# Two-block mixer and expert kernel: gate columns of the second block as fp32 products in four column tiles

## The chip, the cores and the metric

The kernel runs on one core of one Trainium2 chip. The metric is the device time of one execution in microseconds, the median of several. Before the change it is 902.6 us (902.14 to 905.36 over three runs).

## The reference

Two blocks over 256 tokens of 1024 features. The first (an RG-LRU and a spatial gating unit, then a hierarchical mixture of 32 experts) isn't touched. The second has two layers; each projects the normalised tokens to 4360 columns and mixes them by attention, retention and an mLSTM. The last 8 of the columns are the input and forget gates of the mLSTM's four heads:

```python
def hybrid_layer(x, norm_w, w_in, ...):
    h = rmsnorm_2(x, norm_w)
    proj = jnp.matmul(h, w_in).astype(jnp.float32)
    (aq, ak, av, ag, bq, bk, bv, bg, cq, ck, cv, co, cg, ci, cf) = jnp.split(proj, cuts, axis=-1)
    ya = merge_heads(moba_attention(aq, ak, av)) * jax.nn.silu(ag)
    yb = head_norm(retention(rotate(bq), rotate(bk), bv), ret_norm_w) * jax.nn.silu(bg)
    qk = jax.nn.silu(causal_dwconv(jnp.concatenate([cq, ck], axis=-1), conv_w, conv_b))
    i_pre = ci.transpose(0, 2, 1) + gb[:C_HEADS][None, :, None]
    f_pre = cf.transpose(0, 2, 1) + gb[C_HEADS:][None, :, None]
    # mlstm takes the cumulative sum of log_sigmoid(f_pre) over the tokens
    yc = mlstm(qk[..., :C_WIDTH], qk[..., C_WIDTH:], cv, i_pre, f_pre) * jax.nn.sigmoid(co)
    yc = head_norm(yc, mlstm_norm_w) * jax.nn.silu(cg)
    return x + jnp.matmul(jnp.concatenate([ya, yb, yc], axis=-1), w_out)
```

The code is cut: splitting into heads, padding and types are left out. `ci` and `cf` are the gate columns, 4352 to 4359.

## The kernel before

One core, each engine with its own queue written out by hand; semaphores order the engines among each other, and an engine runs its queue strictly in order. After the experts (until about 591 us) comes the second block, `second_block`, with the functions `second_sp`, `second_pe`, `second_act`, `second_pool` and `second_dve`, each of them looping over the layers l = 0, 1.

The projection's weights lie in HBM as "units" of 256 columns, 22 a layer with the output matrix (`NU`). A unit holds 8 row blocks (k = 0 to 7) of 128 rows. Features lie on partitions, tokens on the free axis: `xT` is 8 x (128 x 256). To multiply in fp32r with near fp32 precision each operand is split: ScalarE copies a piece of the weights to a rounded high half (`high(l, u)`, line 1358), VectorE subtracts it from the original to get the low half (`low(l, u)`, line 1366), both in the order of the list `PIECES`; `high(l, u)` and `low(l, u)` do all pieces up to unit u that aren't done yet. The tokens, scaled by the norm's weights, are split in the same way to `HH` and `HL`. TensorE then does three fp32r products for each k (line 1476). `tile(l, u, j)` is 128 columns of unit u, 24 products of 128x128 weights with 256 tokens. The norm's per-token factor comes later, from `rs`, when results leave PSUM.

Unit 2 (`U_ROWS`) holds the gate columns: 8 real ones, padded to 128 (input gates at columns 0 to 3, forget gates at 32 to 35). It is loaded as 128 columns (512 KB), halved like the others (piece `(U_ROWS, 0)`) and multiplied in `tile(l, 2, 0)`. Its result is read by VectorE's `gate_chain` (line 2038 on, lines 2041 and 2042 first), which computes log-sigmoid, cumulative sum and running maximum on 4 partitions. The chain's end (line 2064) is what `stabilisers` on TensorE (lines 1563 and 1564) waits for.

The order of work around it, in each layer. TensorE: the pair of units 0 and 1 (8 steps), the sums of squares (line 1541), `spread_pe` (line 1558, which waits for the root's diagonal `rt` of VectorE, line 2206), `tile(l, 2, 0)`, unit 3 (`U_CO`) in two halves, units 4 and 5 by token (`by_token`, line 1500), unit 6's first half, `stabilisers`, unit 6's second half, `m_rows`, and so on to `r_scores` (line 1635, four 32-row tiles at once), the attention values by token (units 10 and 11, line 1500 again) and the output. ScalarE in layer 0: `high(0, 3)`, the root of the norm (line 1811), `high(0, 5)`, `gate_start`. In layer 1: `high(1, 2)`, the root, `high(1, 5)` (so the halves of unit 3 and then of 4 and 5), `gate_start`. VectorE in layer 0: `low(0, 3)`, the root's reciprocals and diagonal, the copy of the spread factor to `rs` (line 2211), two `conv_in` (line 2251), `low(0, 4, 0)`, two steps of the gate chain, `low(0, 4)`, and so on. In layer 1: `low(1, 2)`, reciprocal and diagonal, `low(1, 3)`, `turn_squares` (four 32x32 transposes of the residual, line 2265), the copy to `rs`, and then as in layer 0. SyncE reloads a unit's slot when the unit four before it is done (`s_unit`).

## Time and profile before

| | |
|---|---|
| median of 3 runs | 902.6 us |
| span of the profiled execution | 901.9 us |
| TensorE busy | 855.3 us (95%) |
| VectorE busy | 416.6 us (46%) |
| ScalarE busy | 301.7 us (33%) |
| second block | from about 591 us to the end |

In the profile PE is TensorE, PEld its weight loads, DVE VectorE, ACT ScalarE, SP SyncE. A group names its line, engine and operation, the tile written and the one read, and the shape. An fp32 product shows as two instructions, an fp32r product as one. Ends of TensorE's instructions are modelled, so products that follow each other are best costed from start to start. In brackets stands how long the engine was idle before, and what released it.

### The profile page before, as it was taken

Reading aid. Unit: us, or ns where it says so; the run is one execution under the profiler, and the core shown is the slowest. Engines: PE = TensorE matmul, PEld = TensorE weight load, DVE = VectorE, ACT = ScalarE, POOL = GpSimd, SP = SyncE. Lnnn points to the kernel's source line nnn. Section 1 sums busy time; section 2 is a strip of 40 time slices with the busy share of each in tenths; the row PEclk is TensorE's granted clock in tenths of the full one; section 3 lists DMA queues with packets and bytes.
Section 4 is the critical chain, followed back from the end, with each engine's and each line's share of the span. In section 5 each row is a group of like instructions: output and inputs, shape, how many; then the busy total and the mean of one; then the engine's idle time right before and its main releaser. Section 6 shows DMA issues by size and latency. Waiting matters only on the chain.

```text
span 901.9 us, 12203 instructions
## 1 busy us (share of the span) xinstructions
PE 855.3 (95%) x5030; PEld 550.6 (61%) x5030; DVE 416.6 (46%) x811; ACT 301.7 (33%) x548; POOL 10.3 (1%) x14
## 2 busy tenths in 40 slices
PE   5999999999998899888998999999999999999997
PEld 3668875344444244423443343389978999897995
DVE  3096954121210112001111111079898888989875
ACT  4253241111111011101110111165746666566663
POOL 0001000000000000000000000000100000010000
PEclk9999999999999999999999999999999999999999
DMA  9999989999999999999999999963425344652532
GB/s 373 423 426 427 396 351 391 394 429 425 428 427 429 426 427 427 427 429 429 426 427 427 429 423 423 418 260 110 174 91 187 141 164 176 184 153 103 182 141 70
DMA packets 34857, 292.96 MB, mean 325 GB/s; under 512 B 11376, under 2 KB 11888, under 8 KB 12912
## 3 DMA queue, kind: packets, MB, share of 16 engines
q1 hardware_dynamic: 34800, 292.16, 79.5%
q8 instruction: 41, 0.67, 0.3%
q14 instruction: 16, 0.13, 0.0%
HBM read 290.05 MB, written 1.05 MB: 323 GB/s over the span
## 4 chain that ended last, share of the span: by engine, by line
PE 71%; DMA 22%; DVE 4%; ACT 1%; issue 1%; SPq 0%; ACTq 0%
PE bank L1476 20%; PE bank L1024 16%; DMA more<-in_expert_w 14%; PE bank L1055 8%; DMA ring<-in_expert_w 7%; PE bank L1500 5%; PE bank L408 3%; PE bank L1519 2%; PE bank L955 2%; PE bank L424 2%; DVE X L378 2%; PE bank L995 2%; DMA ring<-in_ada_w 2%; PE bank L451 2%; PE bank L1676 1%; PE bank L1702 1%
## 5 line engine op out<-in xcount | busy, mean ns | idle before, releaser
L1024 PE MATMUL bank<-ring,xg 128*64 128x512 f32 x760 | 229.4, 607 | 14.2 <-DMA ring<-in_expert_w 14.2
L1476 PE MATMUL bank<-HH,halves 128*128 128x256 f32 x848 | 162.8, 288 | 0.0
L1024 PEld LDWEIGHTS bank<-ring,xg 128*64 128x64 f32 x760 | 71.2, 140 | 133.5 <-issue 109.0
L1476 PEld LDWEIGHTS bank<-HH,halves 128*128 128x128 f32 x848 | 134.5, 191 | 4.5 <-issue 3.5
L1024 PE MATMUL bank<-more,xg 128*64 128x512 f32 x256 | 113.8, 594 | 7.2 <-DMA more<-in_expert_w 7.2
L1476 PE MATMUL bank<-HL,halves 128*128 128x256 f32 x424 | 119.9, 283 | 0.0
L1142 DVE TENSOR_TENSOR X<-X,bank 128x512 f32<-128x512 f32 x16 | 11.0, 688 | 226.3 <-PE bank L1024 226.3
L1055 PE MATMUL bank<-ring,X 128*64 128x512 f32 x384 | 114.3, 595 | 0.7 <-ACT X L1095 0.7
L1366 DVE TENSOR_TENSOR halves<-raw,halves 128x1024 fp32r<-128x1024 f32 (+1 forms) x84 | 91.9, 1129 | 6.2 <-ACT halves L1358 6.2
L1155 DVE SCALAR_TENSOR_TENSOR ygL<-bank,small,ygH 128x512 fp32r<-128x512 f32 x32 | 24.0, 751 | 136.1 <-ACT ygH L1102 136.1
L1476 PEld LDWEIGHTS bank<-HL,halves 128*128 128x128 f32 x424 | 81.2, 191 | 0.7 <-issue 0.5
L1358 ACT ACTIVATE halves<-raw 128x1024 fp32r<-128x1024 f32 (+1 forms) x84 | 78.4, 978 | 1.2 <-DMA raw<-in_units 1.2
L1055 PEld LDWEIGHTS bank<-ring,X 128*64 128x64 f32 x384 | 35.2, 137 | 46.3 <-issue 43.4
L1102 ACT ACTIVATE ygH<-bank,small 128x512 fp32r<-128x512 f32 x32 | 22.0, 687 | 123.2 <-PE bank L1055 123.2
L1024 PEld LDWEIGHTS bank<-more,xg 128*64 128x64 f32 x256 | 34.0, 137 | 46.0 <-issue 34.3
L1066 ACT ACTIVATE xg<-bank,modc 128x256 f32<-128x256 f32 x32 | 13.5, 472 | 139.4 <-PE bank L955 133.8
L1055 PE MATMUL bank<-more,X 128*64 128x512 f32 x128 | 56.6, 595 | 2.1 <-DMA more<-in_expert_w 1.4
L1083 ACT ACTIVATE X<-bank 128x512 f32<-128x512 f32 x16 | 9.6, 597 | 105.8 <-PE bank L1024 105.8
L1500 PE MATMUL bank<-halves,HH 128*128 128x512 f32 x128 | 41.8, 408 | 0.0
L995 PE MATMUL bank<-PT,ygH 128*128 128x256 f32 x128 | 32.7, 293 | 0.4 <-DVE ygL L1155 0.4
L1055 PEld LDWEIGHTS bank<-more,X 128*64 128x64 f32 x128 | 16.9, 137 | 23.6 <-issue 20.0
L995 PE MATMUL bank<-PT,ygL 128*128 128x256 f32 x128 | 31.2, 281 | 0.0
(361 smaller groups left out, 1220.5 us busy)
## 6 DMA issues: line engine op xcount, KB each, us to landing
ring<-in_expert_w SPq DMA_DIRECT2D x63, 2048.0 KB, 26.6
more<-in_expert_w SPq DMA_DIRECT2D x22, 2048.0 KB, 27.1
raw<-in_units SPq DMA_DIRECT2D x38, 1024.0 KB, 4.9
ring<-in_ada_w SPq DMA_DIRECT2D x10, 2048.0 KB, 20.8
ring<-in_expert_w SPq DMA_DIRECT2D x17, 1024.0 KB, 27.9
ring<-in_w_in SPq DMA_DIRECT2D x3, 2048.0 KB, 34.8
more<-in_ada_w SPq DMA_DIRECT2D x2, 2048.0 KB, 27.7
ring<-in_w_out SPq DMA_DIRECT2D x2, 2048.0 KB, 21.6
```

The source lines that it names most:

```text
L378: dve.scalar_tensor_tensor(a, w[:, k, :], cs[:, k:k + 1], a, ALU.mult, ALU.add).then_inc(s_fma, 1)
L408: t = pe.matmul(ps[:, T * j:T * j + T], w[:, k, 128 * (first + j):128 * (first + j) + 128], rhs[:, k, :], start=k == 0, stop=k == 7)
L424: t = pe.matmul(bank[4 + u][:, T * j:T * j + T], w[:, k, 256 * u + 128 * j:256 * u + 128 * j + 128], hT[:, k, :], start=k == 0 and j == 0, ...
L995: t = pe.matmul(bank[ACC[a]][:, T * k:T * k + T], part(y[:, d:d + 128]), part(PT[n % 2][:, :]), start=n == 0 and k == 0 and j == 0, stop=n ...
L1024: t = pe.matmul(bank[3 + i][64 * x:64 * x + 64, :], xg[q % 2][:, k, o + 64 * x:o + 64 * x + 64], w[:, k, :], start=k == 0, stop=k == 7)
L1055: t = pe.matmul(bank[5 + a][64 * x:64 * x + 64, :], aT[:, f, 64 * x:64 * x + 64], place(at[x])[:, 4 * a + f, :], start=f == 0, stop=f == 3)
L1102: act.activation(part(ygH[:, 512 * a:512 * a + 512]), bank[5 + a][:, :], ACT.Copy, scale=weight[n % 2]).then_inc(s_ygh, 1)
L1155: dve.scalar_tensor_tensor(part(ygL[:, h]), bank[5 + a][:, :], weight[n % 2], ygH[:, h], ALU.mult, ALU.subtract).then_inc(s_ygl, 1)
L1358: act.activation(part(hi), src, ACT.Copy).then_inc(s_hi, 1)
L1366: dve.tensor_tensor(part(lo), src, hi, ALU.subtract).then_inc(s_lo, 1)
L1476: t = pe.matmul(ps[:, T * j:T * j + T], part(x[:, k, 128 * j:128 * j + 128]), part(y[:, k, :]), start=first and a == 0, stop=last and a == ...
L1500: t = pe.matmul(v3(ps[j][:, :], 2), part(x[:, k, 128 * j:128 * j + 128]), part(y), start=k == 0 and a == 0, stop=k == 7 and a == 2, skip_g ...
```

## The change

The gate columns leave the fp32r scheme. The array of units keeps for `U_ROWS` 292 numbers a row: 8 row blocks of 32 weight columns (8 real ones, the others zero) and a 0/1 matrix of 128 x 36. Five things change in each layer:

- ScalarE and VectorE no longer split unit 2. VectorE instead multiplies its 8 x 32 columns by the norm's weights (`gate_weigh`), at the head of its layer.
- TensorE does `gate_parts` after the pair and before `spread_pe`: for each k one whole fp32 product of 32 weight columns with `xT[:, k]`, in column tile k mod 4, so that four partial sums of two row blocks each lie on partitions 0, 32, 64 and 96.
- ScalarE copies them to SBUF (`gate_copy`), in layer 0 after `high(0, 3)` and both roots, in layer 1 after `high(1, 1)` and the root; in both before `high(l, 5)`.
- TensorE adds them by one product with the 0/1 matrix (`gate_sums`), between the two halves of unit 3. The signal that unit 2 is done (`s_unit`) comes from this product.
- `tile(l, 2, 0)` goes. In layer 1, `high(1, 2)` and `low(1, 2)` become `high(1, 1)` and `low(1, 1)`.

```diff
-          [(u, i) for i in range(0 if l else 1, 4) for u in (0, 1)] + [(U_ROWS, 0)]
+          [(u, i) for i in range(0 if l else 1, 4) for u in (0, 1)]
...
-            return p["units"][U // NU, U % NU][:, 0:1024 if U % NU == U_ROWS else 2048]
+            return p["units"][U // NU, U % NU][:, 0:GATES if U % NU == U_ROWS else 2048]
...
+                def gate_parts(l):
+
+                    w = gate_weights(l)[0]
+                    ps = start(l, U_ROWS)
+                    pe.wait_ge(s_gw, l + 12)
+                    if l:
+                        pe.wait_ge(s_xo, 4)
+                    else:
+                        pe.wait_ge(s_add, 8)
+                    for k in range(8):
+                        o = 32 * (k % 4)
+                        t = pe.matmul(ps[o:o + 32, 0:T], w[:, k, :], xT[:, k, :], start=k < 4, stop=k >= 4, tile_position=(0, o))
+                    t.then_inc(s_gcT, 1)
+
+                def gate_sums(l):
+                    pe.wait_ge(s_gabs, 5 * l + 1)
+                    pe.matmul(unit_bank(l, U_ROWS)[0:36, T:2 * T], gate_weights(l)[1], X1[:, 1, 0:T], start=True, stop=True).then_inc(s_unit, 1)
...
+                    gate_parts(l)
                     spread_pe(11 if l else 6, 0)
                     pe.wait_ge(s_hl, 8 * l + 8)
-                    tile(l, 2, 0)
                     tile(l, U_CO, 0)
+                    gate_sums(l)
                     tile(l, U_CO, 1)
...
+                def gate_copy(l):
+                    act.wait_ge(s_gcT, 2 * l + 1)
+                    act.activation(X1[:, 1, 0:T], unit_bank(l, U_ROWS)[:, 0:T], ACT.Copy).then_inc(s_gabs, 1)
...
                         scale_root(mean, s_rs, 3)
+                        gate_copy(l)
                         high(l, 5)
                     else:
...
-                        high(l, 2)
+                        high(l, 1)
                         scale_root(bank[6][:, 0:2], s_st2, 2)
+                        gate_copy(l)
                         high(l, 5)
...
+                def gate_weigh(l):
+                    w = gate_weights(l)[0]
+                    scale = col("nw2", 8, 8) if l else gw
+                    dve.wait_ge(*unit_arrival(NU * l + U_ROWS))
+                    dve.tensor_tensor(w, w, scale.unsqueeze(2).broadcast_to([128, 8, 32]), ALU.mult).then_inc(s_gw, 1)
...
                     one = scale(l)
+                    gate_weigh(l)
                     if l == 0:
                         low(l, 3)
                         take(one, 3)
                     else:
-                        low(l, 2)
+                        low(l, 1)
                         take(one, 1)
                         low(l, 3)
                         turn_squares()
```

## Rows read from the trace of the kernel before

**Rows 1.** The page, part 1: busy time, share of the span, instructions of each engine.

```profile
PE 855.3 (95%) x5030; PEld 550.6 (61%) x5030; DVE 416.6 (46%) x811; ACT 301.7 (33%) x548; POOL 10.3 (1%) x14
```

**Rows 2.** Waits of TensorE, 595 to 902 us: total, times, longest.

```profile
PE bank L1558 <- DVE rt L2206: 0.6, 1, 0.6
```

**Rows 3.** The chain that ended last, second block: start, length, what.

```profile
631.74 0.31 PE bank L1563 x2
...
644.10 0.80 PE bank L1617 x8
...
659.76 1.52 PE bank L1635 x32
...
662.50 3.00 PE bank L1500 x12
...
759.74 0.43 PE bank L1558 x2
760.17 8.63 PE bank L1476 x72
...
782.58 0.31 PE bank L1563 x2
...
813.17 2.79 PE bank L1500 x12
```

**Rows 4.** Windows: stretch, length, busy PE, PEld, DVE, ACT, POOL, granted clock, DMA.

```profile
760.00:783.00 23.00, 23.00 (x149) 20.96 (x147) 22.21 (x41) 12.26 (x18) 0.00 (x0) 1.00 0.45 133
783.00:830.00 47.00, 47.00 (x350) 38.95 (x351) 43.05 (x78) 27.62 (x46) 2.98 (x4) 1.00 0.47 138
```

**Rows 5.** Timeline of VectorE, layer 0.

```profile
608.89 0.42 DVE L2211 COPY rs<-bank 128x256 f32<-128x256 f32 x1 [0.79 <-PE bank L1558]
...
611.76 0.41 DVE L2041 TENSOR_TENSOR X<-bank,rs 4x256 f32<-4x256 f32 x1
...
630.38 0.41 DVE L2064 TENSOR_TENSOR X<-X 4x256 f32<-4x256 f32 x1
...
642.40 1.25 DVE L2106 SCALAR_TENSOR_TENSOR X<-bank,X 128x384 f32<-128x384 f32 x2 [3.43 <-ACT X L1843]
...
661.14 1.22 DVE L1366 TENSOR_TENSOR halves<-raw,halves 128x1024 fp32r<-128x1024 f32 x1
```

**Rows 6.** Timeline of TensorE, layer 0: start, length, instruction, idle before.

```profile
607.29 0.28 PE L1476 MATMUL bank<-HH,halves 128*128 128x256 f32 x1
608.16 0.70 PE L1558 MATMUL bank<-rt,cst 128*128 128x256 f32 x2 [0.59 <-DVE rt L2206]
```

**Rows 7.** Timeline of VectorE, layer 1.

```profile
755.16 2.36 DVE L1366 TENSOR_TENSOR halves<-raw,halves 128x1024 fp32r<-128x1024 f32 x2 [0.33 <-ACT halves L1358]
757.44 2.48 DVE L2265 STREAM_TRANSPOSE yT<-xT 128x512 f32<-128x512 f32 x4
760.21 0.42 DVE L2211 COPY rs<-bank 128x256 f32<-128x256 f32 x1 [0.29 <-PE bank L1558]
...
763.08 0.41 DVE L2041 TENSOR_TENSOR X<-bank,rs 4x256 f32<-4x256 f32 x1
...
764.51 2.34 DVE L1366 TENSOR_TENSOR halves<-early,halves 128x1024 fp32r<-128x1024 f32 x2
...
781.37 0.41 DVE L2064 TENSOR_TENSOR X<-X 4x256 f32<-4x256 f32 x1
...
811.59 1.22 DVE L1366 TENSOR_TENSOR halves<-raw,halves 128x1024 fp32r<-128x1024 f32 x1
```

**Rows 8.** Timeline of ScalarE, layer 1.

```profile
754.08 2.00 ACT L1358 ACTIVATE halves<-raw 128x1024 fp32r<-128x1024 f32 x2
...
798.74 0.36 ACT L1847 ACTIVATE scr<-bank 128x256 f32<-128x256 f32 x1
```

**Rows 9.** Experts' stage: a wait of TensorE (timeline), and that stretch's window.

```profile
427.06 8.78 PE L1024 MATMUL bank<-ring,xg 128*64 128x512 f32 x30 [2.70 <-DMA ring<-in_expert_w]
...
426.00:430.00 4.00, 2.94 (x8) 0.82 (x10) 0.00 (x0) 0.00 (x0) 0.00 (x0) 0.70 0.97 414
```

More of the change, by code:

```diff
@@ L48 @@
     0, 2, 3, 4, 6, 8, 9, 10, 12, 13, 14, 15, 16, 18, 22)
+GATES = 8 * 32 + 36
 BY_TOKEN = (U_BV, U_BV + 1, U_AV, U_AV + 1)
 PIECES = [(l, u, i) for l in range(2) for u, i in
-          [(u, i) for i in range(0 if l else 1, 4) for u in (0, 1)] + [(U_ROWS, 0)]
+          [(u, i) for i in range(0 if l else 1, 4) for u in (0, 1)]
           + [(U_CO, 0), (U_CO, 1)]
@@ L169, in unit_place @@
                 return (early0, early1)[U % NU - 4][:, :]
-            return raw[U % 4][:, 0:1024 if U % NU == U_ROWS else 2048]
+            return raw[U % 4][:, 0:GATES if U % NU == U_ROWS else 2048]
         def unit_source(U):
-            return p["units"][U // NU, U % NU][:, 0:1024 if U % NU == U_ROWS else 2048]
+            return p["units"][U // NU, U % NU][:, 0:GATES if U % NU == U_ROWS else 2048]
         def unit_signal(U):
@@ L1306, in rows_of @@
             def rows_of(u, i):
-                if u == U_ROWS:
-                    return 0, 8
                 if u < 2:
@@ L1317, in split_of, with gate_weights @@
                 k, c = rows_of(u, i)
-                w = 128 if u == U_ROWS else T
-                return U, [v3(x[:, 0:8 * w], 8)[:, k:k + c, :] for x in (unit_place(U), hi4[U % 4], lo4[U % 4])]
+                return U, [v3(x, 8)[:, k:k + c, :] for x in (unit_place(U), hi4[U % 4], lo4[U % 4])]
+            def gate_weights(l):
+                there = unit_place(NU * l + U_ROWS)
+                return v3(there[:, 0:256], 8), there[:, 256:GATES]
             def whole(l, u, k):
@@ L1483, in tile @@
                     for i, k in enumerate(order):
-                        if j == 0 and i % 4 == 0 and (u != U_ROWS or i == 0):
+                        if j == 0 and i % 4 == 0:
                             pe.wait_ge(*made(l, u, k))
                         t = products(l, u, j, k, ps, i == 0, i == 7)
-                    if j == 1 or u == U_ROWS:
+                    if j == 1:
                         t.then_inc(s_unit, 1)
+                def gate_parts(l):
[13 more added lines that the diff above has]
+                    pe.matmul(unit_bank(l, U_ROWS)[0:36, T:2 * T], gate_weights(l)[1], X1[:, 1, 0:T], start=True, stop=True).then_inc(s_unit, 1)
                 def by_token(l, u):
@@ L1824, in gate_start @@
                     act.activation(ra, rf, ACT.Abs).then_inc(s_gabs, 1)
-                    act.wait_ge(s_gabs, 4 * l + 1)
+                    act.wait_ge(s_gabs, 5 * l + 2)
                     act.activation(re, ra, ACT.Exp, scale=-1.0).then_inc(s_gabs, 1)
@@ L2040, in gate_chain @@
                     dve.wait_ge(s_unit, U + 1)
-                    dve.tensor_tensor(ri, unit_bank(l, U_ROWS)[0:4, 0:T], rs[0:4, :], ALU.mult).then_inc(s_gate, 1)
-                    dve.tensor_tensor(rf, unit_bank(l, U_ROWS)[32:36, 0:T], rs[32:36, :], ALU.mult).then_inc(s_gate, 1)
+                    dve.tensor_tensor(ri, unit_bank(l, U_ROWS)[0:4, T:2 * T], rs[0:4, :], ALU.mult).then_inc(s_gate, 1)
+                    dve.tensor_tensor(rf, unit_bank(l, U_ROWS)[32:36, T:2 * T], rs[32:36, :], ALU.mult).then_inc(s_gate, 1)
                     yield
@@ L2047, in gate_chain @@
                     yield
-                    dve.wait_ge(s_gabs, 4 * l + 2)
+                    dve.wait_ge(s_gabs, 5 * l + 3)
                     for _ in log1p_dve(re, ra, rw_, rv, s_gate, g + 4):
@@ L2067, in row_lows @@
                 def row_lows(l):
-                    dve.wait_ge(s_gabs, 4 * l + 3)
+                    dve.wait_ge(s_gabs, 5 * l + 4)
                     dve.tensor_tensor(part(rMl[0:4, 0:T]), rM, rMh[0:4, 0:T], ALU.subtract).then_inc(s_gate, 1)
-                    dve.wait_ge(s_gabs, 4 * l + 4)
+                    dve.wait_ge(s_gabs, 5 * l + 5)
                     dve.tensor_tensor(part(rBl[0:4, :]), rB, rBh[0:4, :], ALU.subtract).then_inc(s_gate, 1)
                 def gate_columns(l):
-                    dve.wait_ge(s_gcT, l + 1)
+                    dve.wait_ge(s_gcT, 2 * l + 2)
                     dve.tensor_copy(gc(l, 0, 8), bank[2][:, 0:8]).then_inc(s_gc, 1)
@@ L2578 @@
     w_in_2 = i["w_in_2"][:, :, order]
-    none = np.zeros((2, 1024, 92), np.float32)
-    w_in_2 = np.concatenate([w_in_2[:, :, 0:4356], none[:, :, 0:28], w_in_2[:, :, 4356:4360], none], 2)
+    gate_rows = np.zeros((2, 128, 2048), np.float32)
+    for rows, a in zip(gate_rows, w_in_2):
+        rows[:, 0:256].reshape(128, 8, 32)[:, :, 0:8] = a[:, 4352:4360].reshape(8, 128, 8).transpose(1, 0, 2)
+        for r in range(128):
+            if r % 32 < 8:
+                rows[r, 256 + r % 4 + 32 * (r % 32 // 4)] = 1
     def loads(w, cuts):
@@ L2600 @@
         "fnr": np.broadcast_to(i["final_norm_w_2"].reshape(1, 1024), (128, 1024)),
-        "units": np.stack([np.concatenate([loads(a, [(at, 128 if u == U_ROWS else T) for u, at in enumerate(UNITS)]),
-                                           loads(b, [(T * u, T) for u in range(4)])]) for a, b in zip(w_in_2, i["w_out_2"])]),
+        "units": np.stack([np.concatenate([loads(a, [(at, T) for at in UNITS[:U_ROWS]]), rows[None],
+                                           loads(a, [(at, T) for at in UNITS[U_ROWS + 1:]]),
+                                           loads(b, [(T * u, T) for u in range(4)])]) for a, rows, b in zip(w_in_2, gate_rows, i["w_out_2"])]),
     }
```

2 lines of the change are left out of this document (removed).

## Prediction

> **What bounds the kernel now.** The page's busy shares come first: TensorE is busy for 95% of the span [rows 1]. The change lies in the second block, from 595 us on, so that stretch is what counts. TensorE's own waits there add up to one of 0.6 us, at `spread_pe` of layer 0 [rows 2]. Everything else in the block's chain of waits is TensorE work back to back [rows 3]. Read alone, this says that any TensorE time removed comes straight off the end. The busy times by stretch say something more: from 760 to 783 us VectorE is busy for 22.21 of 23 us, and from 783 to 830 for 43.05 of 47 [rows 4]. So TensorE is the bound there with VectorE hardly less full. The reader has to ask of each place how long before TensorE needed it VectorE had it ready.
>
> Four such margins carry the argument. Layer 0, `stabilisers`: VectorE's last step of the gate chain begins at 630.38 and takes 0.41 [rows 5], TensorE comes at 631.74 [rows 3], margin 0.95. Layer 0, the token-wise attention values: the half of piece (11,0) is done at 662.29 (661.14 + 1.15; of the 1.22 shown some 0.07 overlaps the next instruction) [rows 5], TensorE starts at 662.50 [rows 3]. With some 0.06 for the signal, estimated from the 0.03 between the end of the spread product (608.16 + 0.70) and VectorE's copy at 608.89 [rows 5, 6], the margin is 0.15. Layer 1, the same place: 811.59 + 1.15 = 812.74 [rows 7] against 813.17 [rows 3], margin 0.37. Between the gate chain's start and these places VectorE works through its queue with one break, 3.43 us at 642.40 [rows 5] in which it waits for ScalarE's exponentials; these stand on ScalarE behind the convolutions' SiLU, which wait for VectorE's taps. A delay of VectorE at the chain's start therefore arrives whole at all of them.
>
> **The part removed.** `tile(l, 2, 0)` was 24 TensorE products. 72 of them take 8.63 us [rows 3], so 24 are 2.88 us a layer, 5.75 us in all. The high half on ScalarE and the low half on VectorE of this unit go too (about 1 us each a layer). In both layers they are done before the root of the norm is there, and both engines then wait for that root (it is TensorE's sums of squares that set it), so I cost their going at nothing. `gate_weigh` (one 256-element product on VectorE, 0.42 by the copy at 608.89 [rows 5]) takes their place and hides there as well. The unit's DMA shrinks from 512 KB to 146 KB (292 columns of 128 rows); its data were in time before.
>
> **The part added on TensorE.** `gate_parts` is 8 fp32 products of 32 weight columns, each 256 wide, on four column tiles. A whole fp32 product of 256 columns costs 0.43 (the one at 759.74 [rows 3]), so eight in series are 3.4 us, four at a time 0.85. No operation of the trace has four column tiles. `r_scores` has four row tiles: its 16 products, 3072 columns, would be 5.1 us in series and 1.28 in fours, and they take 1.52 (at 659.76 [rows 3]). Edges and loading then cost 0.24, and I take 0.85 + 0.24 = 1.1 us for `gate_parts` (call it G). The ends: 1.0, and 3.7 if column tiles of 32 do not overlap at all. Column tiles of 64 do overlap in twos: the 8 instructions of 4 products with 768 columns take 0.80 where series would be 1.28 (at 644.10 [rows 3]). Two at a time would make G 2.0. I take four because row tiles do so, and because tiles of 64 reach the full factor that their width allows. `gate_sums` is one product, 0.43 on TensorE. TensorE's own account is then -2.88 + 1.1 + 0.43 = -1.35 a layer.
>
> The Trainium skill, "TensorE: Matmul & The Clock Gate", section "Measured speedup vs the span model", gives 3.07 times for four row tiles and 2.38 for three column tiles, less than full width. The trace agrees in kind, 5.1/1.52 = 3.4 for row tiles. By its 3.07, an estimate, G would be 1.1, and the sum would not move.
>
> **Layer 0, step by step.** The pair's last product starts at 607.29 and TensorE would take the next at 607.41. It now stands idle until 608.16 for the root's diagonal [rows 6]. `gate_parts` fills that and runs until 608.51, so `spread_pe` and VectorE's copy of it are 0.35 late. Next, the gate chain on VectorE used to find its unit done when it came to it, at 611.76 [rows 5]. The unit is now done only when `gate_sums` is: 608.51 + 0.43 + 2.88 (unit 3, first half) = 611.82, and 0.70 for the product to be seen (as the one at 608.16 [rows 6]), 612.52, VectorE at 612.55. The wait on `s_unit` stands in VectorE's queue before `low(l, 4)` and all that follows; so the queue is **0.8 late** from here. TensorE meanwhile is 2 us ahead, and loses it: at `stabilisers` it has to wait for 630.79 + 0.8 + 0.06 = 631.65, against 631.74 before. At the token-wise values VectorE is 0.8 late with a margin of 0.15. Layer 0 costs **+0.65** and gains nothing. ScalarE's copy stands ahead of `high(0, 5)`, and waits until about 608.7; the first piece behind it needs 1.0 more and is there by 610.1, while VectorE wants it 1.2 before its gate chain, at 611.76 - 1.2 + 0.35 = 610.9.
>
> **Layer 1.** Here the wait that the change adds stands at a worse place. Before, ScalarE went from the root straight to the high halves of unit 3 (`U_CO`), at 754.08, in 2.00 us [rows 8], and VectorE made the low halves at 755.16 and turned the squares from 757.44 [rows 7]. Those halves are taken in `high(l, 5)`, and `gate_copy(l)` now stands before it. `gate_copy` waits for `gate_parts`, which TensorE issues only after all 8 steps of the pair, at 759.74 at the latest (the spread product starts there [rows 3]; I count from 759.58, the last product's start plus its step of 0.12). So ScalarE waits with unit 3 behind it: parts issued by 760.68, seen at 760.85 to 760.9, copy 0.3 (a 256-wide one is 0.36 and overlaps the next by 0.1 [rows 8]), high halves from 761.2 instead of 754.08, **7.1 late**. Who waits for that: VectorE's `low(l, 3)`, in its queue before `turn_squares` and before `rs`. Low halves from 762.28, squares from 764.56 (they were 2.28 after the halves), 2.48 for them [rows 7], copy to `rs` at 767.07. It was at 760.21 [rows 7], with 0.29 of waiting in it. VectorE is **6.86 late** there, and at the gate chain, 763.08 before [rows 7]. `gate_sums` is no further delay: unit 3's first half starts at about 763.5, and the sums are seen by 767.2, well ahead of 769.9.
>
> What is late next on TensorE. Unit 3 waits for its low half, 761.1 to 763.5: 2.4 idle. It is through at 763.5 + 2.88 + 0.43 + 2.88 = 769.7, and the half of unit 5 that the token-wise values want first was done at 764.51 + 1.17 [rows 7], now 772.5: 2.8 idle. `stabilisers` wants the gate chain, done at 781.37 + 0.41 [rows 7] + 6.86 + 0.06 = 788.7, and was run at 782.58 [rows 3]: +6.1 there, so the last idle (shared with unit 6's half) is 6.1 + 1.35 - 2.4 - 2.8 = 2.2. The narrowest margin behind it is the 0.37 at 813.17, so the shift grows to 6.86 - 0.37 = **+6.5**. No idle of TensorE is left behind these places that could give any of it back.
>
> **Sum.** +0.65 + 6.5 = +7.15 on the span of 901.9, 909.05. The median of the three runs is 902.6, 0.7 above that span, and I keep this distance: **909.7 us**. With G from 1.0 to 2.0 the two layers follow it one for one: 909.5 to 911.5.
>
> **Rivals.** (a) The sums on TensorE show through: the copy on ScalarE holds nothing up, VectorE turns its squares at 757.44 as before, and layer 0's 0.59 of idling is filled. Then -1.35 x 2 - 0.4 = -3.1, 899.5, faster than before. It would need unit 3 halved ahead of the copy; in layer 0 that is so, in layer 1 the order of the queue speaks against it, and in both layers so does VectorE's full queue. (b) VectorE catches up: only TensorE's direct wait for unit 3 counts, 2.4 - 1.35 = +1.05 in layer 1 and +0.65 in layer 0, 904.3. VectorE would have to find idle time between 760 and 783, and it had 0.8 us there in all [rows 4]. (c) Column tiles of 32 overlap less: in twos 911.5, in series (G 3.7) 914.9. (d) The clock: TensorE's idle stretches of 2.4 and 2.8 us are new in this block. After one of 2.70 us, until 427.06, the granted clock was 0.70 over the four microseconds from 426 [rows 9], so at the lower of its two levels (1.2 of 2.4 GHz) for part of them: 30% of 4 us, 1.2 us of full-speed work lost. Work between the new idle stretches has 2.8 and 2.2 us of idling behind it and absorbs that; a fall that reaches behind `stabilisers` would show, 910.9.
>
> **How the numbers follow.** Forecast 0.62; (c) 0.14 (in series 0.04 of it); (d) 0.08; (b) 0.08; (a) 0.06; 0.02 for a faster time than (a) gives. A difference of over 0.5% is 4.5 us, about what a measurement can tell: 898.1 and 907.1 are the limits. Slower: forecast, (c) and (d), 0.84. Same: (a) and (b), 0.14. Faster: 0.02. The range is the forecast with 1.5 us of error in VectorE's delay and margins, and (c) in twos and (d) above: 907.0 to 912.5, leaving out (a), (b), series and a rest, 0.2.
>
> **What the new profile would show.** Right: in layer 1 a wait of ScalarE of some 6 us just before a 128x256 copy out of the bank; VectorE's transposes at about 765 rather than 757 (add 0.65); TensorE waits of more than 2 us before unit 3 and before units 4 and 5, and waits at `stabilisers`; in layer 0 `stabilisers` at the same time as before within 0.3 us. `gate_parts` from first start to the spread product shows G. Wrong: transposes at 758, or a VectorE that idles for microseconds between the conversion of units 4 and 5 and `stabilisers`, would mean (a) or (b).

## The result, and the profile after

| | before | after | ratio, 95% interval |
|---|---|---|---|
| median, first set | 901.77 us (6 runs) | 912.44 us (6 runs) | 1.0104 [1.0089, 1.0119] |
| median, second set | 902.5 us | 910.62 us (5 runs) | 1.0076 [1.0048, 1.0103] |
| span of the profiled execution | 901.9 us | 909.1 us and 907.4 us | |

The kernel is slower by about 1%. The forecast was 909.7 with a range of 907.0 to 912.5, so the first median lies at its very edge. The sum made against the profiled span was 909.05, and the span came out at 909.1. That agreement is in part luck, as the parts show below.

The profile now says plainly what the profile before only hinted at. The page's busy line, for the kernel after:

```profile
PE 856.1 (94%) x5018; PEld 545.7 (60%) x5018; DVE 414.6 (46%) x811; ACT 300.6 (33%) x548; POOL 10.3 (1%) x14
```

There are 12 instructions fewer on TensorE than in [rows 1] and the same 811 on VectorE. TensorE's waits in the second block, 595 us to the end, after (total, times, longest):

```profile
PE bank L1478 <- DVE halves L1370: 3.5, 3, 2.2
PE bank L1583 <- DVE X L2097: 2.1, 2, 1.1
PE bank L1520 <- DVE halves L1370: 2.1, 1, 2.1
PE bank L1637 <- DVE X L2139: 0.4, 1, 0.4
PE bank L1655 <- DVE scr L2152: 0.2, 1, 0.2
```

One wait of 0.6 us [rows 2] has become 8.3 us, all of it for VectorE. Where they come from is seen on the three queues in layer 1. ScalarE, after (start, length, instruction, idle before):

```profile
761.54 0.38 ACT L1845 ACTIVATE X<-bank 128x256 f32<-128x256 f32 x1 [6.63 <-PE bank L1503]
761.82 1.99 ACT L1362 ACTIVATE halves<-raw 128x1024 fp32r<-128x1024 f32 x2
```

L1845 is `gate_copy`: it stands idle for 6.63 us until `gate_parts` (L1503) is through, and unit 3's high halves start behind it, at 761.82 instead of 754.08 [rows 8]. VectorE, after:

```profile
762.90 2.36 DVE L1370 TENSOR_TENSOR halves<-raw,halves 128x1024 fp32r<-128x1024 f32 x2 [7.33 <-ACT halves L1362]
765.18 2.48 DVE L2298 STREAM_TRANSPOSE yT<-xT 128x512 f32<-128x512 f32 x4
767.59 0.38 DVE L2244 COPY rs<-bank 128x256 f32<-128x256 f32 x1
...
770.34 0.41 DVE L2074 TENSOR_TENSOR X<-bank,rs 4x256 f32<-4x256 f32 x1
```

It idles for 7.33 us, then works without a break, and the gate chain (L2074) starts at 770.34 where it was 763.08 [rows 7]. TensorE, after:

```profile
760.40 1.07 PE L1503 MATMUL bank<-xT,raw 128*32 128x256 f32 x16
761.40 0.70 PE L1578 MATMUL bank<-rt,cst 128*128 128x256 f32 x2
764.27 0.36 PE L1478 MATMUL bank<-HH,halves 128*128 128x256 f32 x1 [2.17 <-DVE halves L1370]
...
773.11 0.70 PE L1520 MATMUL bank<-halves,HH 128*128 128x512 f32 x2 [2.12 <-DVE halves L1370]
...
786.44 0.39 PE L1478 MATMUL bank<-HH,halves 128*128 128x256 f32 x1 [0.74 <-DVE halves L1370]
...
789.19 0.35 PE L1583 MATMUL bank<-cst,X 4*128 4x4 f32 x2 [1.05 <-DVE X L2097]
```

Four stops in layer 1: for unit 3, for units 4 and 5, for unit 6 and at `stabilisers`, 6.1 us in all. The window from 760 to 783 shows the same from above: TensorE 18.71 us busy of 23, where it was 23.00 [rows 4].

```profile
760.00:783.00 23.00, 18.71 (x116) 15.19 (x116) 19.72 (x32) 12.04 (x16) 0.00 (x0) 1.00 0.36 104
```

**How durations are compared from here on.** The experts' stage ends at a slightly different time in each execution. So I measure the second block by itself, from the start of its first whole products (16 fp32 products right behind the experts) to the end of the span. Before: 591.61 to 901.9, 310.29 us. The kernel after: 589.91 to 909.1, 319.19, or +8.9. The second profile of the kernel after: 589.74 to 907.4, 317.66, or **+7.4**. The two differ by a spell at the lower level of TensorE's clock in layer 0, which belongs to the last section. So the profile that hit 909.05 did so with an experts' stage 1.7 us shorter and a slow spell 1.5 us long.

Such spells fall into layer 0 of some profiles below as well. So I also measure layer 1 by itself, from the first product of the mLSTM's norm in layer 0 to the same product in layer 1. In the kernel before that is 812.05 - 661.37 = 150.68 us:

```profile
661.37 1.10 PE L1659 MATMUL bank<-scr,late 128*128 128x512 f32 x2
...
812.05 1.13 PE L1659 MATMUL bank<-scr,late 128*128 128x512 f32 x2
```

In the kernel after (L1679) it is 819.06 - 662.12 = 156.94 and, in the second profile, 817.34 - 660.39 = 156.95: **+6.3** in both.

### The profile page after: what moved, and what is told of

Its sections match the earlier page's. It is cut to its first block, busy times and chain, and to the rows that moved or that the text cites. A ratio compares the mean times of both kernels' runs of the same rounds, so it can differ in the third digit from the quotient of the medians.

```text
span 909.1 us, 12179 instructions
## 1 busy us (share of the span) xinstructions
PE 856.1 (94%) x5018; PEld 545.7 (60%) x5018; DVE 414.6 (46%) x811; ACT 300.6 (33%) x548; POOL 10.3 (1%) x14
## 3 DMA queue, kind: packets, MB, share of 16 engines
HBM read 289.30 MB, written 1.05 MB: 319 GB/s over the span
## 4 chain that ended last, share of the span: by engine, by line
PE 60%; DMA 22%; DVE 13%; ACT 2%; issue 2%; SPq 0%; DVEq 0%; ACTq 0%
PE bank L1026 16%; DMA more<-in_expert_w 14%; PE bank L1478 13%; PE bank L1057 8%; DMA ring<-in_expert_w 7%; PE bank L410 3%; DVE halves L1370 3%; PE bank L1520 3%; PE bank L1539 2%; PE bank L957 2%; PE bank L426 2%; DVE X L380 2%; PE bank L997 2%; DMA ring<-in_ada_w 2%; PE bank L453 2%
## 5 line engine op out<-in xcount | busy, mean ns | idle before, releaser
L1026 PE MATMUL bank<-ring,xg 128*64 128x512 f32 x760 | 234.6, 603 | 12.0 <-DMA ring<-in_expert_w 12.0
L1478 PE MATMUL bank<-HH,halves 128*128 128x256 f32 x816 | 158.3, 289 | 3.5 <-DVE halves L1370 3.5
L1478 PEld LDWEIGHTS bank<-HH,halves 128*128 128x128 f32 x816 | 130.0, 191 | 9.7 <-issue 6.9
L1026 PE MATMUL bank<-more,xg 128*64 128x512 f32 x256 | 119.9, 622 | 8.1 <-DMA more<-in_expert_w 8.1
L1478 PE MATMUL bank<-HL,halves 128*128 128x256 f32 x408 | 115.3, 283 | 0.0
L1370 DVE TENSOR_TENSOR halves<-raw,halves 128x1024 fp32r<-128x1024 f32 (+1 forms) x82 | 89.7, 1126 | 13.3 <-ACT halves L1362 13.3
L1478 PEld LDWEIGHTS bank<-HL,halves 128*128 128x128 f32 x408 | 78.2, 192 | 0.7 <-issue 0.5
L1362 ACT ACTIVATE halves<-raw 128x1024 fp32r<-128x1024 f32 (+1 forms) x82 | 76.2, 976 | 1.1 <-DMA raw<-in_units 1.1
L1026 PEld LDWEIGHTS bank<-more,xg 128*64 128x64 f32 x256 | 35.9, 143 | 47.9 <-issue 37.1
L1520 PE MATMUL bank<-halves,HH 128*128 128x512 f32 x128 | 41.9, 408 | 2.2 <-DVE halves L1370 2.1
```

Of the source, the lines that this page charges most:

```text
L1026: t = pe.matmul(bank[3 + i][64 * x:64 * x + 64, :], xg[q % 2][:, k, o + 64 * x:o + 64 * x + 64], w[:, k, :], start=k == 0, stop=k == 7)
L1362: act.activation(part(hi), src, ACT.Copy).then_inc(s_hi, 1)
L1370: dve.tensor_tensor(part(lo), src, hi, ALU.subtract).then_inc(s_lo, 1)
L1478: t = pe.matmul(ps[:, T * j:T * j + T], part(x[:, k, 128 * j:128 * j + 128]), part(y[:, k, :]), start=first and a == 0, stop=last and a == ...
L1520: t = pe.matmul(v3(ps[j][:, :], 2), part(x[:, k, 128 * j:128 * j + 128]), part(y), start=k == 0 and a == 0, stop=k == 7 and a == 2, skip_g ...
```

## The experiments

**The kernel after once more.** No edit: a second profile, and a time on the same chip as the next runs.

> The changed kernel once more, for a second profile of layer 0. The first one had TensorE's clock at its lower level from about 606 to 609 us, which made the four-tile products 1.87 us long there against 1.04 in layer 1, and the spread product behind them 1.15 against 0.43. Theory A (the fall belongs to the new order of work in layer 0: it follows the sums of squares, two columns wide, and comes as the products of 32 weight columns begin): the fall is there again, layer 0 costs 2 to 3 us from the end of the sums of squares to the attention values by token, and the time is 911 to 913. Theory B (it was chance, as the falls in the experts' stage are): no fall in this profile, layer 0 costs 0.7 to 1.0 us and the profiled time is below 911 by 1.5 us for the same start of the block.

Measured 910.62, ratio 1.0076 [1.0048, 1.0103], block +7.4. Its waits are those shown above, but for that of L1520, which is 0.6 us. There is no fall of the clock in layer 0 this time, and layer 0 costs 0.89 us, as worked out below: theory B. This profile serves for the split by layer in the next section.

**The wait alone, in the kernel before.** ScalarE waits in layer 1 for the pair's product, with nothing else changed:

```diff
                         scale_root(bank[6][:, 0:2], s_st2, 2)
+                        act.wait_ge(s_unit, NU + 2)
                         high(l, 5)
```

> The kernel before with that wait alone: in layer 1 ScalarE waits until units 0 and 1 are through before it makes the high halves of unit 3; nothing else is changed. Theory: high halves 5.7 us later (759.8 instead of 754.1), transposes and the copy of the spread factor 5.4 later, and all of it reaches TensorE less the 0.37 of margin: +5.0, about 906.8, although TensorE does not wait for unit 3 itself (its low half is there by 762.0, TensorE comes at 763.0). Rival (only TensorE's direct wait for unit 3 counts): no change, 901.8.

Measured 907.52, ratio 1.0046 [1.0028, 1.0064], +4.2 us; block +6.1, with a spell at the lower clock in it. Layer 1 by itself is 816.51 - 660.87 = 155.64, or +5.0, as expected. VectorE of this kernel, layer 1:

```profile
760.34 2.36 DVE L1366 TENSOR_TENSOR halves<-raw,halves 128x1024 fp32r<-128x1024 f32 x2 [6.03 <-ACT halves L1358]
762.62 2.48 DVE L2266 STREAM_TRANSPOSE yT<-xT 128x512 f32<-128x512 f32 x4
765.03 0.39 DVE L2212 COPY rs<-bank 128x256 f32<-128x256 f32 x1
...
767.79 0.41 DVE L2042 TENSOR_TENSOR X<-bank,rs 4x256 f32<-4x256 f32 x1
```

One wait on ScalarE, without the new products, does most of the damage. Here TensorE never waits for unit 3 itself, since `tile(1, 2, 0)` covers it; it waits for units 4 and 5 (2.3) and further on (1.1 and 0.8). So the loss is a late VectorE queue, and not a TensorE that lacks unit 3.

**The wait taken away, in the kernel after.** Unit 3 is halved ahead of the copy in layer 1:

```diff
                         scale_root(bank[6][:, 0:2], s_st2, 2)
+                        high(l, 3)
                         gate_copy(l)
```

> The changed kernel with one line moved: in layer 1 ScalarE makes the high halves of unit 3 before it waits for the partial gate sums, not after. Theory (the queue behind ScalarE's copy is the cost of layer 1): the gate chain on VectorE is then held by the gate sums' signal alone, at 764.7 + 0.7 = 765.4 in the times of the first profile instead of 770.3, so the kernel is 4.9 us faster than the changed one, about 907.5. Rival (the cost of layer 1 is TensorE's own, its clock or the four-tile products): the time stays at 912.

Measured 906.47, ratio 1.0036 [1.0015, 1.0056], against 910.62 for the kernel after on the same chip: 4.2 us come back of some 7. Layer 1 by itself is 816.86 - 664.69 = 152.17, so 1.5 us are left there of 6.3. VectorE's turn of the squares begins at 168.2 us from the start of the block (760.73 - 592.54), where it was 175.3 in the first profile of the kernel after. What is late next takes its place: the gate chain.

```profile
768.12 0.41 DVE L2075 TENSOR_TENSOR X<-bank,rs 4x256 f32<-4x256 f32 x1 [0.54 <-PE bank L1508]
```

VectorE is there, and waits 0.54 for `gate_sums` (L1508), which comes only after unit 3's first half. Counted from the start of the block, the chain begins at 175.6 us (768.12 - 592.54), where it was 171.5 before and 178.9 in the second profile of the kernel after. Not all of these 4.1 us belong to layer 1: layer 0 of this profile has a slow spell. Its norm product comes at 72.15 (664.69 - 592.54), where it was 69.76 before and 70.65 in the second profile of the kernel after. So about 0.9 of the 4.1 is layer 0's own cost, 1.5 the spell, and some 1.7 are what the late `gate_sums` leaves in layer 1.

**Less work for TensorE alone.** In the kernel before, unit 2 gets one of its three terms, which takes 16 of 24 products, 1.92 us a layer, off TensorE and moves nothing else. The kernel leaves out the two terms with a low half, so its gates are less exact:

```diff
-                    for a, (x, y) in enumerate(((wh, hi), (wh, lo), (wl, hi))):
+                    terms = ((wh, hi),) if u == U_ROWS else ((wh, hi), (wh, lo), (wl, hi))
+                    for a, (x, y) in enumerate(terms):
...
-                                      stop=last and a == 2, skip_group_check=True)
+                                      stop=last and a == len(terms) - 1, skip_group_check=True)
```

> The kernel before with only the first of the three products of each row block in the gate tile (8 products for 24 in each layer; the terms with a low half are left out, so the gates are less exact). TensorE loses 16 x 0.12 = 1.9 us of work a layer and nothing else changes. Theory (VectorE, with margins of 0.15 and 0.37 us, is the bound behind it): 0.5 us faster, 901.3. Rival (TensorE is the bound, as its 100% busy share says): 3.8 us faster, 898.0.

Measured 903.48, ratio 0.9993 [0.9975, 1.0011]; block -0.2. So 3.8 us less work on an engine that is busy for 95% and hardly waits gained nothing. Waits of TensorE in this kernel, second block:

```profile
PE bank L1564 <- DVE X L2065: 2.1, 2, 1.0
PE bank L1559 <- DVE rt L2207: 0.6, 1, 0.6
PE bank L1618 <- DVE X L2107: 0.4, 1, 0.4
PE bank L1636 <- DVE scr L2120: 0.2, 1, 0.2
```

Most of the removed work has turned into waits for VectorE, 2.7 us of them new, the largest 1.0 at `stabilisers` (L1564) in each layer; that is the 1.92 less the margin of 0.95 that the prediction read there in layer 0. VectorE was less than 2 us ahead of TensorE at each of these places.

**The same with VectorE relieved.** In addition one reciprocal over 4 partitions in each layer's gate chain becomes a multiplication. The kernel leaves the reciprocal out, so the gates' values are wrong, while the order of the work stays:

```diff
-            dve.reciprocal(w, z).then_inc(signal, 1)
+            if z.shape[0] == 4:
+                dve.tensor_scalar(w, z, 0.4, None, ALU.mult).then_inc(signal, 1)
+            else:
+                dve.reciprocal(w, z).then_inc(signal, 1)
```

> b_short, and in the gate chain the 1.74 us reciprocal on 4 partitions is replaced by a product with a constant of 0.28 us (the gates are then wrong in value, the order of the work stays). VectorE gets 1.46 us of air a layer ahead of its tight places, TensorE loses no further work. Theory (VectorE binds once TensorE is relieved): now TensorE's removed work shows, up to the margins of 0.15 + 1.46 = 1.6 and 0.37 + 1.46 = 1.8 us: 3.4 us faster than before, about 899. Rival (the removed products cost nothing in the first place, or something else binds): as b_short, the time of before.

Measured 900.04, ratio 0.9958 [0.9942, 0.9974], block -3.0. Waits of TensorE in this kernel:

```profile
PE bank L1562 <- DVE rt L2210: 0.6, 1, 0.6
PE bank L1639 <- DVE scr L2123: 0.2, 1, 0.2
```

About 1.5 us less on VectorE a layer set 2.8 us of the 3.8 free. This pair of runs is the clearest evidence that the block has two bounds, TensorE and VectorE, about a microsecond apart.

**The change put in a better order.** All of the change is kept, and only its places in the queues differ. ScalarE, layers 0 and 1:

```diff
                         scale_root(mean, s_rs, 3)
+                        high(l, 5, 0)
                         gate_copy(l)
...
                         scale_root(bank[6][:, 0:2], s_st2, 2)
+                        high(l, 3)
                         gate_copy(l)
```

TensorE, layer 1 behind the sums of squares, and then layer 0:

```diff
-                        take(both, 4)
+                        gate_parts(l)
+                        take(both, 2)
+                        spread_pe(11, 0)
+                        take(both, 2)
+                        gate_sums(l)
...
-                    gate_parts(l)
-                    spread_pe(11 if l else 6, 0)
+                    if l == 0:
+                        gate_parts(l, range(0, 4))
+                        spread_pe(6, 0)
+                        gate_parts(l, range(4, 8))
```

The code is cut: in layer 0 `gate_sums` also moves into the middle of unit 3's first half.

> The changed kernel with its steps in other places: layer 1 halves unit 3 before the copy, does the partial products before the pair's last 4 steps, spread in the midst of them, the sums right behind them; layer 0 does four of the partial products before the spread product (in the 0.59 us of idling) and four behind it, and the sums after 4 of the 8 steps of unit 3. VectorE is then hardly later than before (0 in layer 0, 0.3 in layer 1 for units 0 and 1, which TensorE finishes 1.0 later). Theory (VectorE binds): TensorE's saving shows only up to VectorE's margins: 0.2 us faster than before, no measurable difference. Rival (TensorE binds): 3.3 us faster than before.

Measured 902.73, ratio 0.9998 [0.9984, 1.0012], block -0.05. So the 7 us were order alone: with parts and sums placed earlier, the change costs nothing, and its 1.35 us a layer on TensorE gain nothing either, as in the run with less work. The waits that are left (1.0 in all at `stabilisers`, 0.4, 0.2) are for VectorE again.

**GpSimd takes two low halves a layer, in that order.** Pieces (5, 1) and (6, 1). The code is cut to GpSimd's part; VectorE skips these pieces:

```diff
+                    for N in range(len(PIECES)):
+                        if PIECES[N][0] == l and pooled(N):
+                            _, (src, hi, lo) = split_of(N)
+                            pool.wait_ge(s_hi, N + 1)
+                            pool.tensor_tensor(part(lo), src, hi, ALU.subtract).then_inc(s_ropp, 1)
```

> c_order with the two low halves a layer on GpSimd as in b_pool: 2.3 us of air on VectorE. Theory: the saving on TensorE now shows, 1.9 in layer 0 (with the filled idle time) and 1.4 in layer 1: 3.3 us faster than before, about 0.36%. Rival (TensorE's products of 32 columns, or the clock, eat the saving): no difference from before.

Measured 908.21, ratio 1.0055 [1.0034, 1.0075]: a miss by 8 us. What should have taken 2.3 us a layer off VectorE held it up instead. GpSimd and VectorE of this kernel, layer 1:

```profile
764.58 4.55 POOL L2068 TENSOR_TENSOR halves<-early,halves 128x1024 fp32r<-128x1024 f32 x1 [114.15 <-ACT halves L1368]
...
770.72 2.39 POOL L2068 TENSOR_TENSOR halves<-raw,halves 128x1024 fp32r<-128x1024 f32 x1 [1.59 <-ACT halves L1368]
```

```profile
766.80 2.47 DVE L677 TENSOR_SCALAR rows<-X 4x256 f32<-4x256 f32 x1
...
771.08 2.30 DVE L683 TENSOR_TENSOR X<-X,rows 4x256 f32<-4x256 f32 x1
```

These two VectorE steps take 0.28 and 0.41 us in layer 0 of the same profile. Each ends just behind GpSimd's piece: 766.80 + 2.47 = 769.27 behind 764.58 + 4.55 = 769.13, and 771.08 + 2.30 = 773.38 behind 770.72 + 2.39 = 773.11. GpSimd's first piece is itself stretched from 2.39 to 4.55, by 2.16, while VectorE does two subtractions of its own (764.51 to 766.80). In these rows the two take turns. TensorE then waits 2.4 us at `stabilisers` in layer 1, and right behind that wait the clock falls (windows, as above):

```profile
784.00:786.00 2.00, 2.00 (x9) 1.98 (x10) 2.00 (x7) 1.52 (x2) 0.00 (x0) 0.50 1.00 365
786.00:788.00 2.00, 2.00 (x11) 2.00 (x10) 2.00 (x4) 0.00 (x0) 0.00 (x0) 0.50 0.75 164
788.00:790.00 2.00, 2.00 (x11) 2.00 (x10) 1.98 (x5) 1.18 (x3) 0.00 (x0) 0.50 0.04 4
```

This is what rival (d) described, a fall that reaches behind `stabilisers`. From `stabilisers` (783.94) to the norm product (816.41) this kernel takes 32.47 us, and the one without GpSimd 29.87. So of the 5.6 us by which the block is longer in this profile, 2.6 are the lower clock, which came with the wait.

**GpSimd in the kernel before.** The same two pieces:

> The kernel before with two of VectorE's low halves a layer (second piece of unit 5 and of unit 6, 1.15 us each) made by GpSimd instead, which is idle there. Theory (TensorE bounds the kernel before, VectorE is only just behind it): no change, within 0.3% of before. Rival (GpSimd's and VectorE's accesses get in each other's way, or GpSimd's halves come too late): slower by 1 to 3 us; each half should take some 2.4 us there, by the product of 1024 numbers a partition that GpSimd does in 2.36.

Measured 905.01, ratio 1.0017 [1.0002, 1.0031]: a small loss, where nothing was expected. GpSimd's two groups of this kernel (busy, mean ns):

```profile
L2031 POOL TENSOR_TENSOR halves<-early,halves 128x1024 fp32r<-128x1024 f32 x2 | 5.4, 2702 | 649.4 <-ACT halves L1364 649.4
L2031 POOL TENSOR_TENSOR halves<-raw,halves 128x1024 fp32r<-128x1024 f32 x2 | 4.8, 2392 | 13.9 <-ACT halves L1364 13.9
```

The first pieces are stretched less here (2702 ns in the mean, where the second pieces take 2392), and the loss is smaller too: layer 1 by itself is +1.1 (813.76 - 661.97 = 151.79). Two VectorE steps less a layer don't pay for the turns it waits.

**The better order, with the logarithm on ScalarE.** ScalarE's Ln takes the place of the 14 steps a layer in which VectorE computes the logarithm of 1 + z over 4 partitions; nothing of the work is left out:

```diff
-                    act.activation(re, ra, ACT.Exp, scale=-1.0).then_inc(s_gabs, 1)
+                    act.activation(re, ra, ACT.Exp, scale=-1.0).then_inc(s_sig, 1)
+                    act.wait_ge(s_sig, 8 + l + 1)
+                    act.activation(ra, re, ACT.Ln, bias=con("one", 0, 1)[0:4, :]).then_inc(s_gabs, 1)
...
-                    for _ in log1p_dve(re, ra, rw_, rv, s_gate, g + 4):
-                        yield
+                    dve.tensor_copy(rw_[:, 0:1], ra[:, 0:1]).then_inc(s_gate, 14)
+                    yield
```

> c_order with the 13 VectorE steps of log(1 + x) in the gate chain (1.74 us reciprocal, 7 polynomial steps and others, some 6 us a layer by their spacing) replaced by one logarithm on ScalarE, which has idle time there; GpSimd has no part in it. Theory (VectorE bound c_order): TensorE's saving shows now, 1.9 us in layer 0 and 1.4 in layer 1: 3.3 us faster than before, -0.36%, and TensorE has no wait on VectorE left at the stabilisers. Rival (the four-tile products or something else on TensorE eats the saving): the time of before, as c_order.

Measured 899.65 (12 runs) against 902.6, ratio **0.9968 [0.9954, 0.9982]**, block -2.9. It beats both the kernel before and the kernel after. Its page:

```profile
PE 853.9 (95%) x5018; PEld 546.9 (61%) x5018; DVE 402.2 (45%) x785; ACT 303.8 (34%) x552; POOL 10.4 (1%) x14
```

VectorE has 12 us less to do, and TensorE has not one wait in the second block. The gain is TensorE's account at last: 2 x 1.35 and, by the size of it, part of the 0.6 before `spread_pe` in layer 0.

**The logarithm on ScalarE, in the kernel before.** The same edit alone:

> The kernel before with the logarithm on ScalarE alone, nothing else. Theory (before the change TensorE is the bound and VectorE just behind it): no change, within 0.2% of before, although VectorE does 6 us less a layer. Rival (VectorE's load costs the kernel before something as well): faster by 1 us or more.

Measured 902.30, ratio 0.9999 [0.9985, 1.0013]. Layer 1 by itself is -0.3 (812.85 - 662.44 = 150.41). Relief of VectorE by itself is worth nothing that these runs can tell, as less work on TensorE by itself was. Only together do they count.

**The same in the kernel after.** The wait on ScalarE is left in place:

> The changed kernel with the logarithm on ScalarE. It splits the cost of layer 1. Theory: what goes through VectorE's queue behind the gate chain goes away; what stays is TensorE's own waits in layer 1 for unit 3 and for the first half of unit 5, which lie ahead of the relieved steps: by token at 772.5 instead of 768.8 is +3.7, less 1.9 in layer 0, where TensorE's saving now shows: 1.8 us slower than before, so some 8 us faster than the changed kernel. Rival (the cost of layer 1 lies ahead of the relieved steps altogether): +6.5 - 1.9 = 4.6 slower than before.

Measured 904.65, ratio 1.0026 [1.0009, 1.0044], block +1.6, where +1.8 was expected. Waits of TensorE in this kernel:

```profile
PE bank L1478 <- DVE halves L1370: 2.2, 1, 2.2
PE bank L1520 <- DVE halves L1370: 0.6, 1, 0.6
```

Layer 0's norm product comes at 67.79 us from the start of the block (659.65 - 591.86), where it was 69.76 before: TensorE's saving shows there, 2.0 us. Layer 1 by itself is 813.86 - 659.65 = 154.21, or +3.5, where +3.7 was expected. So of the 6.3 us that layer 1 costs in the kernel after, 3.5 are TensorE's stops for the halves of unit 3 and of units 4 and 5, less its own saving, and 2.8 came through VectorE's full queue behind them. The time also lies within 0.4 of the 904.3 of rival (b), but by chance: (b) had +0.65 in layer 0 and +1.05 in layer 1.

**The order of the column tiles.** Neighbouring products go to the same tile (0, 0, 1, 1, ...) instead of in turn (0, 1, 2, 3, 0, ...):

```diff
-                        o = 32 * (k % 4)
+                        o = 32 * (k // 2)
...
```

> The changed kernel with its eight partial products in the order tile 0, 0, 1, 1, 2, 2, 3, 3 instead of 0, 1, 2, 3, 0, 1, 2, 3: the sums are the same. Theory (four column tiles run at once, in order): two products of one tile can't overlap, the next pair's first can: five rounds of 0.43, so 2.1 us instead of 1.04 for the eight in layer 1 (at the full clock), and layer 1 1.1 us longer. Rival (tiles of 32 columns overlap in some other way, say by faster single products): the order makes no difference, 1.04.

One execution, 908.79, span 907.5; layer 1 by itself is +6.3, as in the kernel after. Rows of TensorE in this kernel, layer 1:

```profile
758.72 1.09 PE L1503 MATMUL bank<-xT,raw 128*32 128x256 f32 x16
759.74 0.70 PE L1578 MATMUL bank<-rt,cst 128*128 128x256 f32 x2
```

From the first of the partial products to the spread product 1.02 us, against 1.00 (760.40 to 761.40) in turn. I expected twice that. The order makes no difference here, so the products overlap although half of them follow one to their own tile. What lets them do so stays open; a run with all eight in one tile, which would tell, was not made.

## Why the prediction was right, and where it was off

**The mechanism and its place held.** ScalarE's wait in layer 1: predicted 7.1 us late, high halves at 761.2 plus 0.65, measured 761.82. VectorE's squares: 765.2 predicted with layer 0's share, measured 765.18. Four waits of TensorE, foreseen as 2.4, 2.8 and 2.2 (unit 6 and `stabilisers` together): measured 2.17, 2.12 and 1.79. `stabilisers` at 788.7 plus 0.65: measured 789.19. The stops add up to 1.3 us less than foreseen, and yet the place came when it should. The idle time in brackets is counted from the modelled end of the product before; from start to start the first stop is 764.27 - 761.40 - 0.43 = 2.44, as foreseen. And TensorE starts again more slowly: from 764.27 to `gate_sums` at 767.31 it takes 3.04 for the half unit that I counted at 2.88. In this profile the earlier start of the block and the slow spell of layer 0 cancel, which is why absolute times agree. The run with the wait alone (+4.2) and the one that takes it away (-4.2) show the cause, and the pair with less work for TensorE, without and with relief of VectorE, shows that it acts through VectorE's margins. `stabilisers` in layer 0 came at the time of before, as foreseen: 629.96 - 589.74 = 40.22 in the second profile of the kernel after, against 40.13 before (631.74 - 591.61).

**Layer by layer**, from the second profile of the kernel after, times counted from the block's start. The products of the mLSTM's norm (L1679, before L1659) stand just ahead of the token-wise values. The chain that ended last, second profile of the kernel after:

```profile
659.56 0.70 DVE scr L2158
...
660.39 1.10 PE bank L1679 x2
661.52 2.98 PE bank L1520 x12
```

The values start at 661.52 - 589.74 = 71.78; before they did at 662.50 - 591.61 = 70.89 [rows 3]. So layer 0 costs **+0.89**, predicted +0.65. The term that was off is the margin. I took 0.15 at the piece that the values need. The chain now goes through VectorE's L2158 into L1679, one step earlier, where there was no more than 0.1 to spare; before, that row ended at 661.22 and its reader started at 661.37. A margin has to be read at every handover, not at the one that looks narrowest. (Of the four margins that the prediction speaks of, it works out three; the one left out, `stabilisers` in layer 1, is 782.58 - 781.37 - 0.41 - 0.06 = 0.74.) VectorE's own delay was right: its gate chain begins at 610.78 - 589.74 = 21.04, before at 20.15 [rows 5], so 0.89 late where I had 0.8.

**Layer 1** in the same profile: the first of layer 1's norm products at 817.34 comes 7.2 late, so layer 1 costs **+6.3**, predicted +6.5. VectorE's gate chain is 7.4 late in all (768.61 - 589.74 against 763.08 - 591.61 [rows 7]), less layer 0's 0.9 is 6.5, predicted 6.86.

**`gate_parts`**: 1.00 to 1.04 us at the full clock, predicted 1.1, the lower bound was 1.0. Rival (c) is out. One of the two reasons given for four at a time doesn't hold: the products on tiles of 64 don't reach the full factor of 2, since 1.28 / 0.80 is 1.6. The other, `r_scores` at 3.4 of 4, was enough. `gate_sums` never held anything up in the kernel after in layer 1; VectorE went from the low half straight into the gate chain at 770.34, as argued.

**From the span to the median** the working was too hopeful. It added 0.7; in fact the medians lie 3.3 (912.44 - 909.1) and 3.2 (910.62 - 907.4) above the profiled spans. Of this, 1.3 is a distance that every execution shows between its time and its span (910.43 and 909.1, 908.75 and 907.4). The other 2 come from the two profiled executions being the fastest of their sets. By ratio the two sets give +9.4 and +6.9 us, and the sum of +7.15 lies between them. Part of the spread is the clock, next.

**Rival (d)** happened, though at the stop for unit 3 it cost nothing. In the second profile of the kernel after, the clock fell after the new idle stretch, from about 764 to 767 us: windows of 2 us (length, busy times, granted clock, DMA):

```profile
762.00:764.00 2.00, 1.46 (x11) 1.49 (x12) 2.00 (x3) 2.00 (x4) 0.00 (x0) 0.91 0.04 8
764.00:766.00 2.00, 2.00 (x11) 2.00 (x11) 2.00 (x5) 1.86 (x2) 0.00 (x0) 0.50 0.00 0
766.00:768.00 2.00, 2.00 (x11) 1.37 (x10) 1.97 (x4) 0.00 (x0) 0.00 (x0) 0.74 0.00 0
```

As argued, the next wait absorbed it: the one for units 4 and 5 was 0.6 instead of 2.12. Of the four profiles with an idle stretch of 2.17 us at this place, three show such a fall (the second of the kernel after, the logarithm on ScalarE in the kernel after, the other order of tiles). The first profile of the kernel after shows a granted clock of 1.00 throughout. It has its fall elsewhere, in layer 0, where little behind it absorbs it (the 1.5 us above), and nothing in the prediction covered that. The fall behind `stabilisers` for which (d) gave a price was seen only with GpSimd's pieces; it cost 2.6 us there, where (d) had 1.2.

## What to carry to other kernels

Before taking work off the engine that is busy all the time, read at each handover how far ahead the next engine is: here 3.8 us less on TensorE gained nothing because VectorE was less than 2 us ahead, and the same cut with 1.5 us of relief on VectorE a layer gained 3.2 us (903.19 to 900.04). A copy that waits for a late result must not stand ahead of work that others wait for. Moving that work ahead of the copy gave back 4.2 us of some 7 here, and moving the producer earlier in its own queue as well turned the loss into none. And relief can cost more than it gives: two pieces a layer moved from VectorE to GpSimd cost 5.5 us, the logarithm moved to ScalarE gained 3.

## What the runs showed of the hardware

**GpSimd and VectorE hold each other up.** A VectorE step on 4 x 256 numbers took 2.47 us instead of 0.28 beside a subtraction on GpSimd, another 2.30 instead of 0.40, and GpSimd's own 4.55 instead of 2.39. The Trainium skill, "Perfetto Trace Analysis", section "Optimizing Scalar/DVE Operations", says that the two share a read port and that offloading between them might not help; these rows agree that the offloading didn't help. The kernel took 5.5 us more than with nothing offloaded (908.21 against 902.73), and in the profile 2.6 us of this are the lower clock behind the longer wait. That the cause is the port is the page's word: the rows show only that one step ends when the other's does.

**The clock can fall with TensorE fully busy.** In 5 of the 14 profiles of this study, of kernels with the change and without it, the granted clock fell in layer 0 right behind the 16 products of two columns (32 instructions) for the sums of squares. The first profile of the kernel after, chain and windows:

```profile
601.76 2.57 PE bank L1561 x24
604.34 1.65 PE bank L1478 x12
605.98 1.87 PE bank L1503 x16
607.85 1.15 PE bank L1578 x2
```

```profile
604.00:606.00 2.00, 2.00 (x19) 1.77 (x23) 0.83 (x6) 0.56 (x2) 0.00 (x0) 0.90 0.03 12
606.00:608.00 2.00, 2.00 (x17) 0.73 (x18) 0.40 (x1) 0.09 (x1) 0.00 (x0) 0.50 0.00 0
608.00:610.00 2.00, 2.00 (x12) 1.82 (x13) 0.93 (x2) 2.00 (x3) 0.00 (x0) 0.74 0.00 0
```

TensorE is busy for the whole six microseconds, and yet the granted clock is 0.50 in the middle window, the lower of its two levels of 1.2 and 2.4 GHz; `gate_parts` takes 1.87 us instead of 1.00. Here it costs 1.5 us by the norm product of layer 0 (72.21 from the start of the block, against 70.65 without a fall), since layer 0 has little behind it to absorb that. The Trainium skill, "TensorE: Matmul & The Clock Gate", section "Part 1: The HAM clock gate", ties the lower level to an engine that has been idle; these rows don't show an idle engine, while the falls behind the idle stretches above fit it. What brings the fall in some executions and not in others is open: the run that would tell, with those products put elsewhere, was not made.

**Eight fp32 products of 32 weight columns and 256 columns each take 1.00 to 1.04 us** on four column tiles, 3.3 to 3.4 times less than the 3.44 of eight in series at 0.43 [rows 3], in whichever order the tiles are visited.
